# Residual norms by halves, the first pair of experts in another order, and tile 0's second-norm transposes inside tile 1's output projection

## The reference

```python
def layer(x, mod, P, l, ctx=None):
    sh1, sc1, g1, sh2, sc2, g2 = jnp.split(mod, 6, axis=-1)
    h = rms_norm(x, P["norm_attn_pre"][l]) * (1 + sc1) + sh1
    a, new_ctx = token_mix(h, P, l, ctx)         # three attention branches, gates, merged @ w_out
    x = x + g1 * rms_norm(a, P["norm_attn_post"][l])
    h = rms_norm(x, P["norm_ffn_pre"][l]) * (1 + sc2) + sh2
    x = x + g2 * rms_norm(moe(h, P, l), P["norm_ffn_post"][l])
    return x, new_ctx
```

## Time and profile before

| | |
|---|---|
| three timed runs | 1734.39, 1735.99, 1736.1 us; median 1735.99 |
| the profiled execution | 1733.67 us, span 1731.8 us |
| PE matmul busy | 1673.7 us, 97% |
| PEld / DVE / ACT / POOL busy | 896.0 / 432.0 / 321.2 / 120.9 us |
| weights' queue | 529.55 MB, 74.2% of 16 engines' time |
| mean granted TensorE clock | 0.992 |
| chain that ended last | PE 91%, DVE 4%, DMA 3% |

### The profile page before, as it was taken

One profiled execution on the slowest core, in us unless ns is written; L12 is line 12 of the kernel. 1 busy time (PEld: TensorE's weight loads), 2 busy tenths in 40 slices (PEclk: granted clock), 3 DMA queues, 4 the chain that ended last, 5 costly groups with the idle time before them and its releaser, 6 DMA issues.

```text
span 1731.8 us, 20996 instructions
## 1 busy us (share of the span) xinstructions
PE 1673.7 (97%) x8091; PEld 896.0 (52%) x8091; DVE 432.0 (25%) x1179; ACT 321.2 (19%) x754; POOL 120.9 (7%) x161
## 2 busy tenths in 40 slices
PE   5999998989999999999999999999899999999997
PEld 3777787543333333333367878784433333333332
DVE  1124344351111111111131444433411111111113
ACT  1000341021111111111120113302111111111111
POOL 3001000010000000001020000001100000000000
PEclk9999999999999999999999999899999999999999
DMA  9994222369999999999999632234799999999993
GB/s 388 393 414 139 98 98 95 130 223 389 427 426 424 425 424 426 425 425 425 420 392 419 259 107 98 76 126 182 270 419 427 425 427 424 425 423 426 424 426 140
DMA packets 60380, 559.87 MB, mean 323 GB/s; under 512 B 12940, under 2 KB 13088, under 8 KB 20352
## 3 DMA queue, kind: packets, MB, share of 16 engines
q1 hardware_dynamic: 45360, 529.55, 74.2%
q0 software_dynamic: 14928, 29.02, 4.8%
HBM read 576.02 MB, written 4.78 MB: 335 GB/s over the span
## 4 chain that ended last, share of the span: by engine, by line
PE 91%; DVE 4%; DMA 3%; issue 1%; ACT 1%; SPq 0%; DVEq 0%; PEldq 0%
PE PS L1037 25%; PE PS L616 13%; PE PS L1061 13%; PE PS L1084 12%; PE PS L509 6%; PE PS L855 5%; PE PS L903 3%; DMA ring<-in_blocks 3%; PE PS L682 2%; PE PS L635 1%; PE PS L941 1%; PE PS L559 1%; PE PS L841 1%; PE PS L745 1%; PE PS L790 1%
## 5 line engine op out<-in xcount | busy, mean ns | idle before, releaser
L1037 PE MATMUL PS<-ring,region 128*64 128x512 f32 x2048 | 450.6, 592 | 1.5 <-issue 1.5
L1037 PEld LDWEIGHTS PS<-ring,region 128*64 128x64 f32 x2048 | 147.3, 137 | 290.3 <-issue 290.1
L616 PE MATMUL PS<-region,ring 128*128 128x256 f32 x1088 | 245.3, 381 | 0.5 <-DMA ring<-in_blocks 0.5
L1084 PE MATMUL PS<-region 128*128 128x512 f32 x512 | 241.0, 594 | 0.0
L1061 PE MATMUL PS<-ring,region 128*64 128x512 f32 x1024 | 235.0, 601 | 0.1
L616 PEld LDWEIGHTS PS<-region,ring 128*128 128x128 f32 x1088 | 203.8, 190 | 34.2 <-issue 6.3
L1752 DVE SCALAR_TENSOR_TENSOR region<-region,PS 128x256 f32<-128x256 f32 x64 | 26.9, 421 | 669.9 <-ACT region L1319 669.9
L509 PEld LDWEIGHTS PS<-const,region 128*128 128x128 f32 (+1 forms) x925 | 107.2, 142 | 131.9 <-issue 73.4
L509 PE MATMUL PS<-const,region 128*128 128x128 f32 (+1 forms) x925 | 139.4, 280 | 28.3 <-DMA region<-in_c 9.7
L1061 PEld LDWEIGHTS PS<-ring,region 128*64 128x64 f32 x1024 | 68.0, 137 | 158.3 <-issue 157.6
L1323 ACT ACTIVATE region<-PS 128x512 f32<-128x512 f32 x128 | 76.4, 597 | 266.7 <-PE PS L1061 266.7
(11 more groups left out here) (260 smaller groups left out, 988.0 us busy)
## 6 DMA issues: line engine op xcount, KB each, us to landing
ring<-in_expert_blocks SPq DMA_DIRECT2D x192, 2048.0 KB, 17.0
ring<-in_blocks SPq DMA_DIRECT2D x120, 1024.0 KB, 19.4
region<-post_rows POOLq DMA_DIRECT2D x8, 512.0 KB, 5.1
h_table<-region POOLq DMA_DIRECT2D x4, 512.0 KB, 4.2
region<-in_w_kvk POOLq DMA_DIRECT2D x2, 640.0 KB, 18.3
region<-in_mla_w_ukv POOLq DMA_DIRECT2D x2, 512.0 KB, 21.6
region<-in_post_pack POOLq DMA_DIRECT2D x2, 512.0 KB, 24.9
region<-h_table,region POOLq DMA_INDIRECT x64, 10.8
```

Source lines behind the costliest of these rows:

```text
L616: last = pe.matmul(PS[:, j % 2, m * T:(m + 1) * T], w[:, k, m * P:(m + 1) * P], hT[:, k, :], start=(k == 0), stop=(k == KC - 1))
L1037: last = pe.matmul(PS[e * CAP:(e + 1) * CAP, 0, :], xe[:, k, e * CAP:(e + 1) * CAP], w[:, k % 4, :], start=(k == 0), stop=(k == KC - 1), s ...
L1084: last = pe.matmul(PS[:, 4 + 2 * t + half, :], hot[:, t * P:(t + 1) * P], og[:, half * HALF:(half + 1) * HALF], start=False, stop=True, sk ...
```

## The change

`sums` gets a column for each half of a row, `row_root` adds the two, and `both_roots` takes two tiles' roots together in nine steps. The product with the gain is made before the root is known (`take_gains`), and root and residual are combined in one instruction by halves (`add_rows`). In the last layer VectorE does all of this for both tiles; GpSimd's addition is gone, and four transfers of half a tile write the output. Layer 1's first norm uses `both_roots`.

Tile 0's transposes stand inside the last half of the output projection, behind step 3. ScalarE takes tile 1's first half sum, then tile 0's modulation, then tile 1's second half sum. The steps of the shared expert are ordered anew around tile 1's router. The last ring release of a pass moves from TensorE's `combine` to ScalarE.

The first pair: gate-up starts on the first half of the inputs, the lists' transposes stand before its step 2, and both halves of pair 1's inputs are transposed before the down product, the second into bank 3.

```diff
-VECTOR_STEPS = 246
+VECTOR_STEPS = (248, 243)
...
-            pool.wait_ge(last_scaled, 1)
-            pool.tensor_tensor(xr[:, 0, :], xr[:, 0, :], moe_scaled[:, 0, :], ALU.add).then_inc(last_ready, 1)
...
+                            if t == 1 and half == 1 and k == 3:
+                                normalised(1, 0, xn2, 0)
...
-                normalised(1, 0, xn2, 0, frees=2)
                 pe.wait_ge(rw_in, (l + 1) * 16)
-                router(0)
+                router(0, frees=2)
                 for half in range(2):
                     token_rows(0, half)
-                shared_gate_up(0, range(3))
+                shared_gate_up(0, range(6))
                 normalised(1, 1, xn2, 6)
-                shared_gate_up(0, range(3, 5))
+                shared_gate_up(0, range(6, 7))
                 logits(0)
                 router(1)
-                shared_gate_up(0, range(5, 6))
+                shared_gate_up(0, range(7, KC))
                 logits(1)
-                shared_gate_up(0, range(6, KC))
...
-                shared_down(0)
+                shared_down(0, range(1))
                 shared_transposes(1)
+                shared_down(0, range(1, 2))
                 release(shared_down(1))
...
-                        pe.wait_ge(xe_ready, done + (2 * g + 2))
+                        if g:
+                            pe.wait_ge(xe_ready, done + (2 * g + 2))
                         for k in range(KC):
+                            if g == 0 and k % 4 == 0:
+                                pe.wait_ge(xe_ready, done + (k // 4 + 1))
...
+                                if g == 0 and k == 2 and e == 0:
+                                    transpose_lists()
...
                         for half in range(2):
+                            if g == 0 and half:
+                                pe.wait_ge(xe_ready, done + 4)
...
-                        bank = 3 if g == 0 and half else 1
+                        bank = 3 if g <= 1 and half else 1
...
-                        if g >= 1:
+                        if g >= 1 and not (g == 1 and half):
...
-                    transpose_lists()
                     gate_up(0)
+                    transpose_inputs(1, 0)
                     transpose_hidden(0)
-                    transpose_inputs(1, 0)
+                    transpose_inputs(1, 1)
                     down(0)
-                    transpose_inputs(1, 1)
...
                 branch_sums(0)
                 residual_sums(0)
-                branch_sums(1)
+                branch_sums(1, (0,))
                 modulate(1, h2T, 0, 0, pre2, modT[:, 24:32, :], KC)
+                branch_sums(1, (1,))
                 take_partials(0)
-                residual_sums(1)
                 for half in range(2):
                     take_rows(0, half)
+                residual_sums(1)
...
+                        if half and g == PAIRS - 1:
+                            act.sem_inc(ring_free, 2)
...
+                def both_roots(i, eps=EPS):
+
+                    var, y, t = (roots[:, n, i:i + 2] for n in range(3))
+                    pair = sums[:, 2 * i:2 * i + 4].rearrange("p (t h) -> p t h", h=2)
+                    dve.wait_ge(sum_done, l * SUMS + 2 * i + 4)
+                    step(ve.scalar_tensor_tensor(out=var, in0=pair[:, :, 0], scalar=D * eps, in1=pair[:, :, 1], op0=ALU.add, op1=ALU.add))
...
+                def take_gains(i, t, rows, rows_in):
+
                     dve.wait_ge(postb_in, (l * 2 + rows_in) * 2 * 16)
+                    for half, cols in enumerate(HALVES):
+                        dve.wait_ge(sum_done, l * SUMS + 2 * i + half + 1)
+                        step.add(ve.tensor_tensor(rows[:, t, cols], PS[:, 4 + 2 * t + half, :], postb[:, t, cols], ALU.mult))
+
+                def add_rows(r, t, rows, done):
+
+                    for half, cols in enumerate(HALVES):
+                        ve.scalar_tensor_tensor(out=xr[:, t, cols], in0=rows[:, t, cols], scalar=r, in1=xr[:, t, cols], op0=ALU.mult, op1=ALU.add).then_inc(done, 1)
...
+                for t in range(2):
+                    take_gains(6 + t, t, moe_scaled, 2)
+                r = both_roots(6)
+                for t in range(2):
+                    add_rows(r[:, t:t + 1], t, moe_scaled, x_ready)
```

More of the change, by code:

```diff
@@ L70 @@
 PAR_ROWS = 68
-SUMS = 8
+SUMS = 16
 ROOT_SCALE = -0.375
@@ L304, in hybrid_layers @@
             sem("hidT_ready"), sem("down_done"), sem("og_ready"), sem("hot_ready"))
-        comb_done = [sem(f"comb_done{t}") for t in range(2)]
+        comb_half, comb_done = ([sem(f"{name}{t}") for t in range(2)] for name in ("comb_half", "comb_done"))
         vector_step = sem("vector_step")
@@ L924, in router @@
                                          start=(k < 2), stop=(k >= KC - 2), skip_group_check=True)
+                        if k == 0 and frees:
+                            release(last, frees)
                     last.then_inc(router_done, 1)
@@ L960, in shared_down @@
                     pe.wait_ge(htok_ready, l * 4 + 2 * t + 2)
-                    for half in range(2):
+                    for half in parts:
                         for f in range(2):
@@ L1087, in combine @@
                                 release(last, frees)
+                            if half == 0 and last_pair:
+                                last.then_inc(comb_half[t], 1)
                         last.then_inc(comb_done[t], 1)
@@ L1327, in _ @@
                     half_tanh(0)
-                    take_inputs(1, 0)
+                    for half in range(2):
+                        take_inputs(1, half)
                     for half in range(2):
                         take_out(0, half)
-                    take_inputs(1, 1)
                     for g in range(1, PAIRS):
@@ L1405, in row_root @@
                 def row_root(i, eps=EPS):
-                    var, y, t = (roots[:, i, n:n + 1] for n in range(3))
-                    dve.wait_ge(sum_done, l * SUMS + i + 1)
-                    step(ve.tensor_scalar(var, sums[:, i:i + 1], D * eps, None, ALU.add))
+                    var, y, t = (roots[:, n, i:i + 1] for n in range(3))
+                    dve.wait_ge(sum_done, l * SUMS + 2 * i + 2)
+                    step(ve.tensor_scalar(var, sums[:, 2 * i:2 * i + 1], sums[:, 2 * i + 1:2 * i + 2], D * eps, ALU.add, ALU.add))
                     step(ve.tensor_scalar(y.bitcast(I32), var.bitcast(I32), -0.5, float(0x5F3759DF), ALU.mult, ALU.add))
@@ L1421, in normalise_x @@
+                def normalise_x(r, t, dst):
                     ve.tensor_scalar(dst[:, t, :], xr[:, t, :], r, ROOT_SCALE, ALU.mult, ALU.mult).then_inc(xn_ready, 1)
-                def add_normalised(i, t, rows, rows_in, done, eps):
-                    r = row_root(i, eps)
+                def take_gains(i, t, rows, rows_in):
                     dve.wait_ge(postb_in, (l * 2 + rows_in) * 2 * 16)
-                    step(ve.scalar_tensor_tensor(out=rows[:, t, :], in0=PS[:, 4 + 2 * t:6 + 2 * t, :].rearrange("p b n -> p (b n)"), scalar=r, in1=postb[:, t, :],
-                                                 op0=ALU.mult, op1=ALU.mult))
-                    ve.tensor_tensor(xr[:, t, :], xr[:, t, :], rows[:, t, :], ALU.add).then_inc(done, 1)
+                    for half, cols in enumerate(HALVES):
+                        dve.wait_ge(sum_done, l * SUMS + 2 * i + half + 1)
+                        step.add(ve.tensor_tensor(rows[:, t, cols], PS[:, 4 + 2 * t + half, :], postb[:, t, cols], ALU.mult))
@@ L1436, in modulate @@
                                          shift[:, c, t:t + 1], ALU.mult, ALU.add).then_inc(h_dve, 1)
-                for t in range(2):
-                    normalise_x(t, t, xn1)
+                if l == 0:
+                    for t in range(2):
+                        normalise_x(row_root(t), t, xn1)
+                else:
+                    r = both_roots(0)
+                    for t in range(2):
+                        normalise_x(r[:, t:t + 1], t, xn1)
                 dve.wait_ge(params_tr, l + 1)
```

95 lines of the change are left out of this document (46 added, 49 removed).

## The result

| | kernel before | kernel changed |
|---|---|---|
| first comparison, median | 1735.19 us (1732.7 to 1736.1, 4 runs) | 1722.7 us (1722.02 to 1725.61, 4 runs) |
| changed kernel timed again | 1733.87 us (1732.28 to 1736.54, 21 runs) | 1719.69 us (1718.31 to 1722.19, 5 runs) |

The ratio is 0.9934 (95% interval 0.9916 to 0.9951), and 0.9922 (0.9909 to 0.9936) the second time: 11.5 and 13.5 us faster by the ratios, with intervals of 8.5 to 14.6 and 11.1 to 15.8 us. 1724.5 us had been forecast.

The account below looks back on a forecast made before the run. TensorE was taken to lead at 15.13 us a pair, transfers nearly level at about 15.6. Gains of 5.1 (layer 0), 4.1 (layer 1) and 2.1 (tail) sum to 11.3 us, subtracted from about 1735.8: 1724.5 us, range 1720 to 1730.

Parts of the forecast that it names:

- The transposes inside the projection: Tile 0's transposes behind step 3 of tile 1's last projection half: 2.4 us of cover, router done 2.6 us earlier.
- the first transposes of inputs: Start of pair 0's input transposes after the first gather: 2.2 us earlier, at 376.9 instead of 379.1.
- rival A: First gather keeps its 6.4 us after the selection; each layer loses 1.0, gain 9.3, or 7.3 if pair 1's also lags; chance 0.17.
- the 2.06: TensorE's wait for pair 0's hidden rows before the down product, expected to stay at 2.06 us.
- The stream: Expert-load transfers in layer 0, expected 4.3 us earlier, between 2.6 and 5.5.
- the load of 399.3: Expert load landing after an unqueued 7.7 us; expected 5.8 earlier by its release but held behind its neighbours.
- a wait for ring blocks of more than 0.8: Sign of being right: TensorE waits more than 0.8 us for ring blocks between 865 and 900.
- The tail: End of the last layer, with half squares, half adds and no GpSimd addition: gain 2.1 us, 1.0 to 2.6.
- 5.1 for layer 0: Layer 0's gain in us, limited at the layer boundary by the block issued at 873.9: slack 1.1 plus 4.3 minus 0.3.
- Rival C: The stream and both gathers follow TensorE fully: gain 13.5, time 1722.3 us; chance 0.10.
- A sign of "wrong": TensorE waiting for expert loads near pair 30, where 1.7 us of slack was expected to hold.
- rival E: Slower through TensorE's half clock after idle waits, 5 us each; three more such stretches give 1739 us; chance 0.05.

Follow-up runs that it names:

- the second profile: The changed kernel run again without edit, for a second profile and timing: 1719.69 us, ratio 0.9922.
- VectorE's addition: Kernel before, with tile 0's last addition on VectorE in place of GpSimd: 1733.44 us, ratio 0.9997.
- the light loads: Expert loads bring 3840 of 4096 columns: 1721.39 us in the changed kernel, 1733.95 us in the kernel before.
- the earlier release: Changed kernel, with pair 0's slots of the second gate-up load released by pair 1's input transposes instead of the hidden rows': 1721.33 us, ratio 0.992.
- the three later edits: To the changed kernel: early release with load behind table writes, 1721.53 us; that plus one more shared step, 1721.89; separately, layer 1's parameters later, 1721.49.
- the old pair: Changed kernel with the first pair's order of before, its waits, bank and ScalarE copies included: 1728.9 us, ratio 0.9966.
- the halves alone: Kernel before with only norms by halves and the new tail; both old orders, tile 0's transposes behind the projection: 1733.0 us, ratio 0.9989.
- the five extra edits: Not listed in the text; apparently, on the changed kernel: slots released earlier, shorter loads, load behind table writes, extra shared step, later parameters: 1721.33 to 1721.89 us.

## Why the prediction was right, and where not

**Right by their steps.** The transposes inside the projection had no wait, and the router of tile 0 ran in 1.1 us. In the terms of before, tile 1's transposes came at 353.6 (forecast 354.0), the rank matmuls at 364.0 (364.25) after 0.81 idle (1.0), the first transposes of inputs at 376.3 (376.9), the first gate-up at 377.7 (378.3), pair 1 at 391.8 (392.25); in layer 1 74.4 to 74.6 us behind the projection where 74.5 followed from the forecast. In layer 0 the first gather landed in time, without a wait of TensorE, so rival A fell. Pair 1's did not quite (0.49 us at 387.97), but the hidden rows then had only 0.92 left of the 2.06 that I had kept for them. In layer 1 of the second profile TensorE waited 0.46 us for the first gather (0.54 before) and 1.30 for pair 1's, ahead of hidden rows that were then ready: about the same loss in another place. No GpSimd addition and no root step over 0.17 us in the tail.

**The stream was mis-sized.** I put the stream of transfers 4.3 us earlier, at most 5.5; that the unqueued load of 399.3 would be held behind its neighbours was right, but I took the few loads in the busy stretch for the whole. Measured from the projection, the landings of the loads behind the one of 379.07 come 4.5, 3.8, 3.9, 3.3 and 5.2 us earlier, and from the seventh on 5.1 to 6.1, up to the end of the pass. This term of my sum, 4.3, is the step that was wrong in size.

I had read too much into the load of 399.3, which landed after 7.7 us. Its successor in the changed kernel is the load of 395.1, which took 10.1. But the 7.7 came with the half clock: in the kernel before with VectorE's addition, at full clock there, the same load is issued 1.5 us nearer to the projection and takes 9.7.

```profile
L357 SPq DMA_DIRECT2D ring<-in_expert_blocks x1: 333/333/333, 395.1 to 395.1; - x1
...
DMA to landing us min/median/max: 10.1/10.1/10.1
```

```profile
L356 SPq DMA_DIRECT2D ring<-in_expert_blocks x1: 333/333/333, 399.6 to 399.6; - x1
...
DMA to landing us min/median/max: 9.7/9.7/9.7
```

From the seventh load to the thirty-second that profile's landings lie within 0.3 us of the kernel before, although its TensorE is 1.5 us earlier. So a gap ahead of the load of 399.3 does not explain the stream. Against the same profile the landings of the second changed profile come 3.6 and 3.4 us earlier at first, 4.4 to 5.5 from the third to the ninth, and mostly about 6 from the tenth on. Why the lead grows from load to load stays open.

So against the profile of before layer 0 is worth not 5.1 but 6.3 plus 1.3 at the boundary, 7.6, in the second profile (5.6 in the first, where 1.7 went to half clock). 1.5 of it are the half clock of before. The sign that I gave for it, a wait for ring blocks of more than 0.8, came: 1.15 and 1.40 at the first block, and in the second profile 1.00 at the later one. The first block was not what bounded the boundary in the profile of before, as the light loads showed.

**The tail** gave 2.5 instead of 2.1: the gain product of the last half runs while the sum is still on its way, and the additions follow each other in 2.74, not 2.88.

**The sum.** 7.6, 4.4 and 2.5 are 14.5, and the rest of the 15.3 us between the profile of before and the second changed one is 0.9 in layer 1's attention, less rounding: there the kernel before had 10.2 us of half clock and the second profile 3.4. Against these two profiles the sum of 11.3 was low by 3. They flatter the change, though: less the 0.9 and the 1.5 of half clock in layer 0, they differ by 12.9, and the timed medians by 12.5 and 14.2. So the gain was forecast 1 to 3 us too small. My own 5.1 for layer 0 was built on the same profile: pair 1's 5.8 there held the half clock, and only the stream's limit kept it lower. With a gain of 12.5 from 1735.19, where I had 11.3 from 1735.8, the time came out 1.8 us under the forecast. The closeness is partly luck: when timed again the changed kernel's median, 1719.69, lies just outside my range of 1720 to 1730, with the kernel before lower as well. Rival C (13.5) was nearer to the mechanism than the forecast.

**A sign of "wrong" came up, in layer 1.** I had named TensorE waiting for expert loads near pair 30 as a sign against me, and looked at layer 0 alone. In the first changed profile the pairs from 22 on take up to 15.65 us instead of 15.13 and cost 1.9 us. It has this gate-up of 7.30 us instead of 7.04, and this load at layer 1's start, issued 65.7 us behind the projection:

```profile
1635.03 7.30 PE L1041 MATMUL PS<-ring,region 128*64 128x512 f32 x32
...
L357 SPq DMA_DIRECT2D ring<-in_expert_blocks x1: 342/342/342, 1231.7 to 1231.7; - x1
...
DMA to landing us min/median/max: 11.4/11.4/11.4
```

The same load in the second profile, issued 65.5 us behind the projection:

```profile
L357 SPq DMA_DIRECT2D ring<-in_expert_blocks x1: 342/342/342, 1226.3 to 1226.3; - x1
...
DMA to landing us min/median/max: 8.7/8.7/8.7
```

That load landed 2.8 us later, all behind it stayed 2 to 3 us later, and at pair 29 the slack between the second gate-up load's landing and its use, 3.5 us into the pair, was 0.0 us. In the second profile it was 0.9, in the kernel before 2.3, with the shorter loads 13.6. The change spends 1.4 us of it in layer 1, because TensorE moved 4.3 us there and the first loads less. Why that one load took longer stays open. It was not the only such case: with the earlier release that load lands 0.3 us too late at pair 29 and the pass loses 0.5, while in the second profile and in those of the three later edits it loses at most 0.1.

**Half clock, rival E,** did not decide. The 3.4 us behind the 2.06 us wait of before are absent in the changed kernel, where that wait is shorter. They are absent as well in most profiles that keep it: of the ten waits of 2.06 us (two layers of the kernel before, of the two profiles of it with an edit elsewhere, of the old pair and of the halves alone) three are followed by half clock. And no busy stretch ahead of the experts has any in the changed kernel's two profiles. What appeared at 265 appeared as well in profiles of the kernel before with an edit elsewhere (the shorter loads, and VectorE's last addition), so it is not the change's.

## What to carry to other kernels

When the leading engine is pulled forward, list the slack of the next resource at its tightest place in every pass, not in one, and take the stream's move from many loads of a second profile, not from the one load that looks free. Before removing a wait, look for the chain that would end just behind it: of the five extra edits here each took its wait away or a landing or issue forward, and none moved the time by what can be measured. Undo the parts of a change one at a time and also leave one alone: here they cost 4.7, 1.8 and 3.7 us of layer 0 singly and 5.7 together, and the halves alone lose 0.8. Look at the granted clock of each stretch before you subtract: 2.9 us of those numbers, and 1.5 of the gain itself, were half clock that another profile does not show.

## What the runs showed of the hardware

- One and the same program had 3.4 or 10.2 us of half clock at the same place of layer 0's attention (near 270), and reached its output projection at 317.7 or 319.8 us. At the boundary a wait of 1.40 us was followed by half clock, and one of 1.15 in the other profile was not; with the shorter loads one of 1.04 was. The same wait of 2.06 us was followed by half clock three times in ten.
- A write of 32 KB landed 1.7 us after its issue ahead of a 2 MB load of another queue and 5.0 us behind one; with the load issued within 0.1 us of the second write, that one took 5.2 and the first 1.7. By the Trainium skill (DMA: Bandwidth & Descriptors, Queues, rings and completion order) each DMA engine takes its queues in turn by packets. Here a small write that was issued 2.5 us behind the load still landed only with the load's end.
